# Grouped attention: the probabilities are normalised on GpSimd ahead of the transposition, in place of turned inverses and a separate gate product

## The reference, cut to what matters

```python
def blocked_attention(q, k, v, scale):
    def one_block(q_blk):
        s = jnp.einsum('bqkgd,bnkd->bkgqn', q_blk, k, preferred_element_type=jnp.float32) * scale
        p = jax.nn.softmax(s, axis=-1).astype(v.dtype)
        return jnp.einsum('bkgqn,bnkd->bqkgd', p, v)
    ...
y_l = (o_l.reshape(h_lat.shape[:2] + (GQA_WIDTH,)) * jax.nn.silu(g_l)) @ w_out
```

## Time and profile before

| | us |
|---|---|
| median of 3 runs | 1908.98 (1907.12 to 1909.59) |
| the profiled execution | 1906.22 |
| its span on the core | 1904.2 |
| TensorE busy in the span | 1707.7 (90%) |
| VectorE busy | 905.8 (48%) |
| ScalarE busy | 821.9 (43%) |
| GpSimd busy | 349.4 (18%) |
| first score matmul of grouped attention | at 403.6 |
| last gate product of grouped attention | at 741.3 |

### The profile page before, as it was taken

One profiled execution on the slowest core, in us unless ns is written; L12 is line 12 of the kernel. 1 busy time (PEld: TensorE's weight loads), 2 busy tenths in 40 slices (PEclk: granted clock), 3 DMA queues, 4 the chain that ended last, 5 costly groups with the idle time before them and its releaser, 6 DMA issues. The chain is left out here.

```text
span 1904.2 us, 28321 instructions
## 1 busy us (share of the span) xinstructions
PE 1707.7 (90%) x10190; PEld 1421.1 (75%) x10190; DVE 905.8 (48%) x2262; ACT 821.9 (43%) x1926; POOL 349.4 (18%) x246
## 2 busy tenths in 40 slices
PE   7699999989999996999698998999588889889696
PEld 3177778879999886666487888998477777777585
DVE  1612212148888887112610101211388888889523
ACT  3222222147777775001311111011188888888312
POOL 0112201001111113111000000000155555554200
PEclk9899999999999998999899999999799999999898
DMA  7622204168000002443322221112333333332422
GB/s 277 243 78 55 78 23 134 66 88 105 15 15 15 15 28 67 156 159 106 144 89 78 88 76 59 45 34 88 98 84 95 94 85 90 86 90 60 177 89 111
DMA packets 112331, 170.56 MB, mean 90 GB/s; under 512 B 49426, under 2 KB 87396, under 8 KB 111972
## 3 DMA queue, kind: packets, MB, share of 16 engines
q1 hardware_dynamic: 112228, 169.15, 29.4%
HBM read 115.65 MB, written 45.55 MB: 85 GB/s over the span
## 5 line engine op out<-in xcount | busy, mean ns | idle before, releaser
L590 DVE TENSOR_TENSOR w_lo<-w_raw,w_hi 128x1024 fp32r<-128x1024 f32 x36 | 45.4, 1262 | 280.4 <-ACT w_hi L534 280.3
L891 PE MATMUL pp<-h_hi,w_hi 128*128 128x512 f32 (+1 forms) x432 | 155.9, 361 | 9.5 <-PEq L124 8.6
L1578 PE MATMUL nTB<-ident,nprob 128*128 128x128 f32 x768 | 133.0, 283 | 32.8 <-DVE pt_mid_lo L1762 10.5
L892 PE MATMUL pp<-h_lo,w_hi 128*128 128x512 f32 (+1 forms) x432 | 153.9, 356 | 0.0
L893 PE MATMUL pp<-h_hi,w_lo 128*128 128x512 f32 (+1 forms) x432 | 153.9, 356 | 0.0
L1339 ACT ACTIVATE prob<-S,nm,qk_inv 128x512 f32<-128x512 f32 (+1 forms) x208 | 146.5, 707 | 7.8 <-DVE nm L1275 7.8
L1578 PEld LDWEIGHTS nTB<-ident,nprob 128*128 128x128 f32 x768 | 88.0, 141 | 77.2 <-DVE pt_mid_lo L1762 29.3
L640 PE MATMUL ppo<-h_hi,w_hi 128*128 128x512 f32 (+1 forms) x320 | 120.3, 376 | 27.1 <-DVE h_lo L576 14.9
L1568 PE MATMUL nS<-k_split,q_split 128*128 128x256 f32 (+2 forms) x320 | 109.0, 368 | 35.7 <-DMA k_swapped<-k_split 25.4
L534 ACT CAST w_hi<-w_raw 128x1024 fp32r<-128x1024 f32 x36 | 37.9, 1052 | 230.4 <-DMA w_raw<-in_ga_w_out 80.0
L1293 DVE TENSOR_TENSOR ptlo<-TB,pthi 128x512 fp32r<-128x512 f32 (+1 forms) x192 | 114.7, 597 | 29.9 <-ACT pthi L1351 28.0
(11 more groups left out here) (219 smaller groups left out, 4940.7 us busy)
## 6 DMA issues: line engine op xcount, KB each, us to landing
wmod<-in_mod_w SPq DMA_DIRECT2D x48, 512.0 KB, 4.8
w_raw<-in_na_w_in SPq DMA_DIRECT2D x16, 1024.0 KB, 5.4
xt_scratch<-xt SPq DMA_DIRECT2D x2, 5120.0 KB, 16.2
k_swapped<-k_split SPq DMA_DIRECT2D x32, 320.0 KB, 4.2
w_raw<-in_ga_w_in SPq DMA_DIRECT2D x9, 1024.0 KB, 5.3
bias_scratch<-in_bias SPq DMA_DIRECT2D x16, 476.2 KB, 17.1
bias_end<-bias_scratch SPq DMA_DIRECT2D x32, 224.0 KB, 4.4
gate_scratch<-g_stage SPq DMA_DIRECT2D x8, 640.0 KB, 3.0
```

Source lines behind the costliest of these rows:

```text
L891: pe.matmul(acc, whi[:, k, ws], hi[:, k, a:a + width], start=(k == 0), stop=False)
L892: pe.matmul(acc, whi[:, k, ws], lo[:, k, a:a + width], start=False, stop=False)
L1578: last = pe.transpose(TB[:, k, b * P:(b + 1) * P], prob[:, p % 4, a:a + P], consts["ident"][:, :])
```

## The change

- A new function `normalise` on GpSimd multiplies a tile of `prob` in place by its own `rec`, in round p + 2, after `reciprocal` and ahead of the transposition. `turn` waits for it (`scaled`) once per tile instead of for the exponential of each chunk.
- `reciprocal` on VectorE is done for each tile, at the end of round p + 2, instead of for each group in odd rounds.
- The two transpositions of `rec` ahead of each product, the buffer `inv` and the copy into it go.
- `out` multiplies the product directly by the gate `g` and waits for the gate's load itself; GpSimd's `gate` goes. SyncE loads the next gate after the former head's last `out`.
- `LAG` is 4 instead of 3, so that transposition, product and `out` come one round later; `TAIL` is 7 instead of 6. The rings of `prob` and of the maxima have six tiles instead of five, counted through the heads (`slot`).

```diff
+    RING = 6
...
-        prob = c.sb("prob", [P, 5, T])
+        prob = c.sb("prob", [P, RING, T])
...
-        inv = c.sb("inv_sums", [P, 256])
...
+        def slot(h, p):
+
+            return (h * GQA_N + p) % RING
...
-        LAG = 3
+        LAG = 4
...
                 def load(h):
-                    at_least(sp, gated, GQA_GROUPS, h, -1)
+                    at_least(sp, od, GQA_GROUPS, h, -1)
...
                 def turn(h, p, k):
                     a, n = key_chunks(p)[k]
                     no = chunk_no(p, k)
-                    at_least(pe, expd, CHUNKS, h, no)
+                    if k == 0:
+                        at_least(pe, scaled, GQA_N, h, p)
                     at_least(pe, lod, CHUNKS, h, no - 2)
...
                     if 0 in blocks:
                         at_least(pe, lod, CHUNKS, h, chunk_no(2 * gr + 1, len(key_chunks(q)) - 1))
-                        at_least(pe, recd, GQA_GROUPS, h, gr)
                         at_least(pe, od, GQA_GROUPS, h, gr - 1)
-                        for s in range(2):
-                            pe.transpose(O[:, 256 + s * P:256 + (s + 1) * P],
-                                         rec[:, q - 1 + s:q + s].broadcast_to([P, P]), consts["ident"][:, :])
...
-                def reciprocal(h, gr):
-
-                    q = (2 * gr) % GQA_N
-                    n = len(key_chunks(q))
-                    at_least(dve, expd, CHUNKS, h, chunk_no(2 * gr + 1, n - 1))
-                    dve.tensor_reduce(tot[:, q:q + 2], sums[:, q:q + 2, 0:n], AX, ALU.add).then_inc(totd, 1)
-                    at_least(dve, totd, GQA_GROUPS, h, gr)
-                    dve.reciprocal(rec[:, q:q + 2], tot[:, q:q + 2]).then_inc(recd, 1)
+                def reciprocal(h, p):
+
+                    q = p % GQA_N
+                    n = len(key_chunks(p))
+                    at_least(dve, expd, CHUNKS, h, chunk_no(p, n - 1))
+                    dve.tensor_reduce(tot[:, q:q + 1], sums[:, q, 0:n], AX, ALU.add).then_inc(totd, 1)
+                    at_least(dve, totd, GQA_N, h, p)
+                    dve.reciprocal(rec[:, q:q + 1], tot[:, q:q + 1]).then_inc(recd, 1)
...
+                    at_least(dve, gl, 1, 16 * head, 15)
                     at_least(dve, pvd, GQA_GROUPS, h, gr)
-                    dve.tensor_copy(inv[:, :], O[:, 256:512]).then_inc(invd, 1)
-                    at_least(dve, invd, GQA_GROUPS, h, gr)
                     dve.tensor_tensor(qk[:, bass.ds(head, 1), tok:tok + 256].rearrange("p a n -> p (a n)"),
-                                      O[:, 0:256], inv[:, :], ALU.mult).then_inc(od, 1)
+                                      O[:, 0:256], g[:, tok:tok + 256], ALU.mult).then_inc(od, 1)
...
-                        if p % 2 == 1 and live((p - 3) // 2, prev, tail):
-                            reciprocal(h, (p - 3) // 2)
+                        if live(p - 2, prev, tail):
+                            reciprocal(h, p - 2)
...
-                        at_least(act, td, CHUNKS, h, chunk_no(p - 5, len(key_chunks(p - 5)) - 1))
+                        at_least(act, td, CHUNKS, h, chunk_no(p - RING, len(key_chunks(p - RING)) - 1))
...
-                def gate(h, gr):
...
-                    at_least(pool, gl, 1, 16 * head, 15)
-                    at_least(pool, od, GQA_GROUPS, h, gr)
-                    pool.tensor_tensor(o, o, g[:, tok:tok + 256], ALU.mult).then_inc(gated, 1)
+                def normalise(h, p):
+
+                    n = GQA_TILES[p % GQA_N][1]
+                    q = p % GQA_N
+                    at_least(pool, recd, GQA_N, h, p)
+                    pr = prob[:, slot(h, p), 0:n]
+                    pool.tensor_scalar(pr, pr, rec[:, q:q + 1], None, ALU.mult).then_inc(scaled, 1)
...
-                        if (p - OUT) % 2 == 0 and live((p - OUT) // 2, prev, tail):
-                            gate(h, (p - OUT) // 2)
+                        if live(p - 2, prev, tail):
+                            normalise(h, p - 2)
```

More of the change, by code:

```diff
@@ L1132, in grouped_attention @@
         g = c.sb("gate_in", [P, T])
-        inv = c.sb("inv_sums", [P, 256])
-        mx, sums = c.sb("mx", [P, 5, 3]), c.sb("sums", [P, GQA_N, 3])
-        top = c.sb("mx_raw", [P, 5])
-        nm, tot, rec = c.sb("nm", [P, 5]), c.sb("tot", [P, GQA_N]), c.sb("rec", [P, GQA_N])
+        mx, sums = c.sb("mx", [P, RING, 3]), c.sb("sums", [P, GQA_N, 3])
+        top = c.sb("mx_raw", [P, RING])
+        nm, tot, rec = c.sb("nm", [P, RING]), c.sb("tot", [P, GQA_N]), c.sb("rec", [P, GQA_N])
         S, TB, O = c.ps("S", [P, S_RING, 512]), c.ps("TB", [P, 2, 512]), c.ps("O", [P, 512])
@@ L1140, in grouped_attention @@
         topd = c.sem("g_max_raw")
-        totd, recd, gated, invd = c.sem("g_total"), c.sem("g_recip"), c.sem("g_gated"), c.sem("g_inv")
+        totd, recd, scaled = c.sem("g_total"), c.sem("g_recip"), c.sem("g_prob_scaled")
         td, hid, lod = c.sem("g_turned"), c.sem("g_pt_hi"), c.sem("g_pt_lo")
@@ L1220, in turn @@
                         last = pe.transpose(TB[:, no % 2, b * P:(b + 1) * P],
-                                            prob[:, p % 5, a + b * P:a + (b + 1) * P], consts["ident"][:, :])
+                                            prob[:, slot(h, p), a + b * P:a + (b + 1) * P], consts["ident"][:, :])
                     last.then_inc(td, 1)
@@ L1267, in biggest @@
                     at_least(dve, qkd, CHUNKS, h, chunk_no(p, k))
-                    dve.tensor_reduce(mx[:, p % 5, k:k + 1], S[:, score_bank(p, k), 0:n], AX, ALU.max).then_inc(mxd, 1)
+                    dve.tensor_reduce(mx[:, slot(h, p), k:k + 1], S[:, score_bank(p, k), 0:n], AX, ALU.max).then_inc(mxd, 1)
                 def negmax(h, p):
@@ L1272, in negmax @@
                     at_least(dve, mxd, CHUNKS, h, chunk_no(p, n - 1))
-                    dve.tensor_reduce(top[:, p % 5:p % 5 + 1], mx[:, p % 5, 0:n], AX, ALU.max).then_inc(topd, 1)
+                    dve.tensor_reduce(top[:, slot(h, p):slot(h, p) + 1], mx[:, slot(h, p), 0:n], AX, ALU.max).then_inc(topd, 1)
                     at_least(dve, topd, GQA_N, h, p)
-                    dve.tensor_scalar(nm[:, p % 5:p % 5 + 1], top[:, p % 5:p % 5 + 1], q_scale(h, p), -1.0,
+                    dve.tensor_scalar(nm[:, slot(h, p):slot(h, p) + 1], top[:, slot(h, p):slot(h, p) + 1], q_scale(h, p), -1.0,
                                       ALU.mult, ALU.mult).then_inc(nmd, 1)
-                def reciprocal(h, gr):
-                    q = (2 * gr) % GQA_N
-                    n = len(key_chunks(q))
-                    at_least(dve, expd, CHUNKS, h, chunk_no(2 * gr + 1, n - 1))
-                    dve.tensor_reduce(tot[:, q:q + 2], sums[:, q:q + 2, 0:n], AX, ALU.add).then_inc(totd, 1)
-                    at_least(dve, totd, GQA_GROUPS, h, gr)
-                    dve.reciprocal(rec[:, q:q + 2], tot[:, q:q + 2]).then_inc(recd, 1)
+                def reciprocal(h, p):
[5 more added lines that the diff above has]
+                    dve.reciprocal(rec[:, q:q + 1], tot[:, q:q + 1]).then_inc(recd, 1)
                 def low(h, p, k):
@@ L1337, in exps @@
                         at_least(act, nmd, GQA_N, h, p)
-                        at_least(act, td, CHUNKS, h, chunk_no(p - 5, len(key_chunks(p - 5)) - 1))
-                    act.activation(prob[:, p % 5, a:a + n], S[:, score_bank(p, k), 0:n], ACT.Exp,
-                                   bias=nm[:, p % 5:p % 5 + 1],
+                        at_least(act, td, CHUNKS, h, chunk_no(p - RING, len(key_chunks(p - RING)) - 1))
+                    act.activation(prob[:, slot(h, p), a:a + n], S[:, score_bank(p, k), 0:n], ACT.Exp,
+                                   bias=nm[:, slot(h, p):slot(h, p) + 1],
                                    scale=q_scale(h - 1, p) if p < 0 else q_scale(h, p),
@@ L1382, in q_low @@
                                        qhi[:, a:a + n], ALU.subtract).then_inc(q_lo, 1)
-                def gate(h, gr):
-                    head = h - 1 if gr < 0 else h
-                    tok = GQA_TILES[(2 * gr) % GQA_N][0]
-                    o = qk[:, bass.ds(head, 1), tok:tok + 256].rearrange("p a n -> p (a n)")
-                    at_least(pool, gl, 1, 16 * head, 15)
-                    at_least(pool, od, GQA_GROUPS, h, gr)
-                    pool.tensor_tensor(o, o, g[:, tok:tok + 256], ALU.mult).then_inc(gated, 1)
+                def normalise(h, p):
[4 more added lines that the diff above has]
+                    pool.tensor_scalar(pr, pr, rec[:, q:q + 1], None, ALU.mult).then_inc(scaled, 1)
                 def body(h, kv, kvp, tail=False):
```

## The result

The change makes the kernel slower: 1926.06 us median (1924.55 to 1927.19) against 1908.05 before, a ratio of 1.0096 with a 95% interval of 1.0078 to 1.0113. The forecast was 1900.0 us, in a range of 1895.5 to 1909. The profiled execution of the changed kernel took 1927.19 us with a span of 1925.3, 21.1 longer than the span before.

What follows compares the result with a forecast made beforehand. TensorE's instruction stream was taken as the bound. Transposes -8.8, `out` wait -1.0, stage end -1.3 and extra lag +1.0 make -10.1; with 1.1 given back, -9.0 us from 1908.98: 1900.0, range 1895.5 to 1909.

Steps and rivals of the forecast that it cites:

- GpSimd: the unknown: On GpSimd, each in-place multiply of 128x1280 by a scalar per partition takes 1.3 us, between bounds of 1.25 and 2.94.
- The new wait and its slack: On TensorE, turns wait for normalise with 2.0 us left in the tightest short rounds; it fits, so costed at nothing.
- The slow rival: On GpSimd, normalise takes 2.9 us and turns wait some 2.4 us per head, giving 1919 us; chance 0.14.
- The sum without the wait: Whole kernel: all costed terms with nothing for turns waiting on GpSimd, 9.0 us less after a give-back of 1.1.
- The third rival: On TensorE, nothing gained: 0.11 us per transpose was hidden in a pipeline bubble, about 1908 us; chance 0.05.
- `out` wait: TensorE's matmuls wait 5.4 us for VectorE's `out` in the stage; 1.0 us of it goes, ends 0 and 5.4.
- the turned inverses: On TensorE, removing 80 transposes of the inverses at 0.11 us each saves 8.8 us.
- VectorE: In grouped attention, VectorE's work falls by 4 us over the stage, to about 34.6 us per head; costed at nothing.
- The second rival: VectorE or ScalarE becomes the bound, leaving a gain of 4 to 5 us, 1904.5 us; chance 0.12.
- The end of the stage: From the last product matmul to the next stage's first work, 1.07 us instead of 2.39, so 1.3 us less.
- The fourth lag: In grouped attention, one more round at start and tail idles TensorE and costs 1.0 us, ends 0.3 and 2.8.
- Behind the last scores: At the tail of grouped attention, more than 18 us after the last scores would show the forecast wrong.

Runs made afterwards that it cites:

- forms: The kernel before, with GpSimd copies and one- and two-input multiplies on spare tiles added ahead of its work for the first head; total time not read.
- n256: The changed kernel with normalise scaling only the first 256 key columns of each tile; 1899.56 us, ratio 0.9949 to the kernel before.

## Why the prediction was wrong

The step that failed is "GpSimd: the unknown". It argued that "the number of input streams is what separates these rows", took 1.3 us from the fastest of the casts (1036 ns at 1024 columns, where the median was 1772), and put the upper bound at the two-input form's 2.94. The instruction takes 3.52, 2.7 times the value taken and beyond the bound. The forms run shows what separates the rows in its place: the operation. A one-input copy takes 1.25 us, a one-input multiply 3.44 to 3.52, a two-input multiply 2.88. The Trainium skill's page "GPSIMD Engine Reference", section 4.1, has one-input work roughly at line rate; the copy agrees (1.25 us for 1280 columns), the multiply does not. Its other figure, in section 3.1, about 2.6 cycles of 1.2 GHz per element, gave an estimate of 2.8 us. The prediction calls that figure general; the section explains it as the floor of two-input work. The multiply's slope from 256 to 1280 columns, (3521 - 922) / 1024 = 2.54 ns, is 3.0 cycles, above it, with one input. The forecast used the page to confirm the cast's row instead of letting the two disagreeing figures raise the rival's chance. And with its price put at nothing, a wait of 27.4 us was missing from the sum.

Point by point, the rest:

- **The new wait and its slack** was right in mechanism, and 2.0 us was the right size for the tightest place: the stage is 0.8 us longer at 1.89 us, 4.4 at 2.32 and 14.3 at 2.85 (table). The waits stood ahead of turns, behind short rounds, as it said. But only the turn behind round 5 had so little; those behind rounds 4, 8 and 9 had 2.4 to 2.7 in n256.
- **The slow rival** named the outcome's direction and mechanism, at 0.14. Its price was somewhat high at its own length (19 us against 14.6), and its length too low: at 3.52 us the change gives 26.5 us more than n256, which with n256's 9.3 under before makes some 17 over it, near the 18 measured. The 1919 of the rival was 7 short.
- **The sum without the wait**, 9.0, was right: n256 has 9.3 (1899.56 against 1908.89), and a head takes 40.2 us where 40.1 was forecast. The third rival falls with it. That the sum is so close is in part luck: the `out` wait fell by 2.8 us more than was taken (below), so the other terms together gave 2.5 less. The 8.8 of **the turned inverses** was not measured by itself. TensorE's busy time in the stage fell from 329.1 to 323.6, by 5.5 us, but overlapping matmuls make this a poor measure of what they cost the stream.
- **VectorE** fell as worked out, and never bound: 34.85 us in n256's stretch of 41.2, which is 34.0 in a head of 40.2, against the forecast's 34.6. The second rival falls. `out` kept its 424 ns while GpSimd ran next to it.
- **The `out` wait** fell from 5.4 us to 1.5 in the change and 1.6 in n256, 3.8 where 1.0 was taken, inside the stated ends.
- **The gate**: its loads landed in 3.8 to 4.3 us in the change, and nothing waited for them.
- **The end of the stage**: the last product matmul starts at 761.02 and the next stage at 762.13, 1.11 us against the 1.07 worked out.
- **The fourth lag**, 1.0: nothing visible with the rest of the change, 3.6 us alone on the kernel before. Neither lies inside its ends of 0.3 and 2.8, but neither run is exact enough to exclude them: the interval of the second is 1.3 to 5.9.
- **Behind the last scores** the change has 18.3 us (743.8 to 762.1), over the 18 that the forecast gave as a sign of being wrong; n256 has 17.1.

So the rest of the sum was near, though not each of its terms, and one instruction with no row of its own turned the sign. The chance of 0.14 for it was too small because the bound behind it was not a bound.

## What to carry to other kernels

When a change puts an instruction on a path with a fixed slack, and no row shows that operation on that engine, treat every other operation's row as a guess, not as an end of the range, and compare the whole span of guesses with the slack: here a slack of 2.0 us lay in the middle of guesses from 1.3 to 2.9, which called for a larger chance than 0.14. When a wait of this kind is found, look first at what releases the late instruction. Here moving a 0.3 us reciprocal half a round ahead was worth 26 us, as much as shortening the 3.5 us instruction itself. Try the other forms of the same arithmetic as well.

## What was not expected of the hardware

- On GpSimd, multiplying a 128x1280 float32 tile by one scalar per partition takes 3.52 us as a one-input instruction, and 2.32 us as a two-input one whose second operand is the same column broadcast. The full two-input form takes 2.88, so the broadcast operand is cheaper than a full one, and both two-input forms are faster than the one-input multiply.
- An immediate in place of the scalar per partition saves 0.07 us of 3.52, and writing to another tile saves nothing.
- No sign that VectorE's and GpSimd's instructions lengthen each other in this stage: in the change `out` stays within 423 to 426 ns with GpSimd at seven tenths, `low` has a median of 691 ns as in n256, and `normalise` is within 3.52 and 3.53 from median to longest.
